# Keys and queries of the differential attention: turning two heads' fp32 rows at once and splitting them behind the turn, against splitting first and turning one head at a time

## What is computed

```
q = (x @ w_q).reshape(B, S, 2, H, Dh) * (Dh ** -0.5)      # H = 8 heads, two maps of Dh = 64
q1, q2 = partial_rope(q[:, :, 0]), partial_rope(q[:, :, 1])
a = softmax(q1 k1^T) - lam * softmax(q2 k2^T)              # causal
o = rms_norm(a @ v) * (1 - lambda_init);  return o @ w_out
```

## Time and profile before

| | |
|---|---|
| three runs | 1014.42 us median (1013.09 to 1014.72) |
| the profiled execution, its time | 1013.32 us |
| its span, first to last instruction | 1011.4 us |
| mean granted TensorE clock | 0.999 |
| busy: PE, DVE, ACT, POOL | 998.2, 664.6, 469.5, 103.7 us |
| differential attention from the query projection to its output | about 740 to 812 us of the span |

### The profile page before, as it was taken

The page is one execution under the profiler, slowest core; times in us unless marked ns, Lnnn a source line. Parts: engine busy times, 40 slices in busy tenths (PEclk is TensorE's granted clock), DMA queues, the critical chain, the costliest instruction groups (busy, mean ns, idle before and its releaser), DMA issues.

```text
span 1011.4 us, 13543 instructions
## 1 busy us (share of the span) xinstructions
PE 998.2 (99%) x5374; PEld 850.5 (84%) x5374; DVE 664.6 (66%) x653; ACT 469.5 (46%) x632; POOL 103.7 (10%) x141
## 2 busy tenths in 40 slices
PE   9999999999999999999999999999998999999997
PEld 7888888888888888888888888888887788888885
DVE  5876763765856667674575567774598877677544
ACT  7544433444864544343443444333468655434430
POOL 0020000222920100000022000000033110000000
PEclk9999999999999999999999999999999999999999
DMA  9866554560223755554447664654459366555431
GB/s 333 295 213 223 199 209 172 195 221 1 87 95 96 249 183 173 212 196 167 167 167 234 217 215 166 207 208 166 167 173 160 126 208 210 165 180 215 146 123 42
DMA packets 80060, 181.58 MB, mean 180 GB/s; under 512 B 3392, under 2 KB 9680, under 8 KB 80016
## 3 DMA queue, kind: packets, MB, share of 16 engines
q1 hardware_dynamic: 73312, 170.21, 48.4%
q0 software_dynamic: 6704, 10.76, 4.4%
HBM read 177.81 MB, written 1.05 MB: 177 GB/s over the span
## 4 chain that ended last, share of the span: by engine, by line
PE 94%; DVE 2%; ACT 2%; DMA 0%; issue 0%; POOL 0%; POOLq 0%; SPq 0%; DVEq 0%; ACTq 0%
PE acc L1479 15%; PE acc L1481 15%; PE acc L1480 15%; PE acc L1579 13%; PE aux L1579 7%; PE acc L1581 7%; PE trb L1579 6%; PE trb L1529 4%; PE aux L1581 4%; PE trb L1581 3%; PE acc L1737 1%; PE acc L1600 1%; PE acc L1597 1%; PE acc L1601 1%; PE aux L1781 1%; ACT norm_gb L782 1%
## 5 line engine op out<-in xcount | busy, mean ns | idle before, releaser
L968 DVE TENSOR_TENSOR w_lo<-raw,w_hi 128x2048 fp32r<-128x2048 f32 x148 | 336.6, 2283 | 174.0 <-ACT w_hi L674 173.9
L674 ACT ACTIVATE w_hi<-raw 128x2048 fp32r<-128x2048 f32 x148 | 280.3, 1902 | 152.4 <-PE acc L1481 124.3
L1579 PE MATMUL acc<-xt,w_hi 128*128 128x512 f32 x576 | 205.0, 395 | 0.0
L1581 PE MATMUL acc<-xt,w_lo 128*128 128x256 f32 x576 | 161.6, 280 | 0.0
L1479 PE MATMUL acc<-w_hi,ht_hi 128*128 128x512 f32 x352 | 137.0, 389 | 0.0
L1481 PE MATMUL acc<-w_hi,ht_lo 128*128 128x512 f32 x352 | 136.8, 389 | 0.0
L1480 PE MATMUL acc<-w_lo,ht_hi 128*128 128x512 f32 x352 | 136.8, 389 | 0.0
L1579 PEld LDWEIGHTS acc<-xt,w_hi 128*128 128x128 f32 x576 | 108.0, 187 | 25.4
L1479 PE MATMUL acc<-w_hi,xt 128*128 128x512 f32 (+1 forms) x320 | 127.3, 398 | 0.2 <-DVE xt L983 0.2
L1481 PE MATMUL acc<-w_hi,xt 128*128 128x512 f32 (+1 forms) x320 | 123.5, 386 | 0.0
L1480 PE MATMUL acc<-w_lo,xt 128*128 128x512 f32 (+1 forms) x320 | 123.4, 385 | 0.0
(11 more groups left out here) (233 smaller groups left out, 1306.8 us busy)
## 6 DMA issues: line engine op xcount, KB each, us to landing
raw<-ffn_gate_up SPq DMA_DIRECT2D x84, 1024.0 KB, 5.2
raw<-ffn_w_down SPq DMA_DIRECT2D x44, 1024.0 KB, 4.9
raw<-w_kv SPq DMA_DIRECT2D x8, 1024.0 KB, 6.2
raw<-w_in SPq DMA_DIRECT2D x6, 1024.0 KB, 5.2
raw<-ffn_gate_up SPq DMA_DIRECT2D x16, 256.0 KB, 6.1
raw<-w_out_a SPq DMA_DIRECT2D x4, 1024.0 KB, 6.0
raw<-w_q SPq DMA_DIRECT2D x4, 1024.0 KB, 5.1
raw<-w_out_b SPq DMA_DIRECT2D x4, 1024.0 KB, 5.5
```

What stands on the lines that cost most here:

```text
L674: act.activation(w_hi[:, slot, 0:k * c], raw[:, slot, 0:k * c], ACT.Copy).then_inc(hi_ready, 1)
L968: dve.tensor_tensor(w_lo[:, slot, 0:k * c], raw[:, slot, 0:k * c], w_hi[:, slot, 0:k * c].bitcast(F32), ALU.subtract).then_inc(lo_ready, 1)
L1579: pe.matmul(bank.rearrange("p (a s) -> p a s", a=2), hi[:, k, cols], xt[:, :, kt, :], start=(kt == 0), stop=False)
L1581: ins = pe.matmul(bank[:, 0:SEQ], lo[:, k, cols], xt_hi[:, kt, :], start=False, stop=(kt == KT - 1))
```

## The change

The rotated fp32 rows are turned as they are, two maps of 64 in one 128x128 block, so a turn of four blocks now carries 8 maps, and there are 8 turns in place of 16. `split_beside` is gone for keys and queries of this mixer. Behind a turn `stacked_high` has ACT write the high parts out of PSUM, in two instructions of 64 partitions (the even maps lie on the upper 64 partitions, the odd ones on the lower 64), and `stacked_low` has DVE write the low parts in two more, each onto the other 64 partitions of the same slot; only then is the bank freed. For odd maps the high part now lies on the lower 64 partitions, in keys and queries alike. `dq` is now `y`, the mixer's output keeps `k_nat` under the name `diff_o`, and a small product moves within `y`. Late turns are one at step 2 and one at step 6, behind the turn of the probabilities; the queries of tile 0 are all turned before the loop. PE's early turns stand before k-steps 1 and 3 of both units of four k-steps, then before query pieces 1 and 3.

```diff
-DIFF_EARLY = [("kr", tok, part) for tok in range(TOKS) for part in range(4)] + [("qr", 0, 0), ("qr", 0, 1)]
-DIFF_LATE = {0: ((("qr", 0, 2),), (("qr", 0, 3),)), 2: ((("qr", 1, 0),), (("qr", 1, 1),)),
-             6: ((("qr", 1, 2),), (("qr", 1, 3),))}
+DIFF_EARLY = [("kr", 0, 0), ("kr", 0, 1), ("kr", 1, 0), ("kr", 1, 1), ("qr", 0, 0), ("qr", 0, 1)]
+DIFF_LATE = {2: ("qr", 1, 0), 6: ("qr", 1, 1)}
...
+        dq = y
+        diff_o = k_nat
+        def stacked(heads, part, tok):
+            at = [(slice(8 * part + r, 8 * part + 8, 2), slice(tok * P, (tok + 1) * P)) for r in range(2)]
+            top, low = slice(0, DH), slice(DH, P)
+            return [(top, heads[top, at[0][0], at[0][1]], heads[low, at[0][0], at[0][1]]),
+                    (low, heads[low, at[1][0], at[1][1]], heads[top, at[1][0], at[1][1]])]
...
             def swap_keys(tok):
                 for half in range(2):
-                    for part in (2 * half, 2 * half + 1):
-                        t = TURN_OF["kr", "diff", tok, part]
-                        pool.wait_ge(tr_free[t % 2], t // 2 + 1)
+                    t = TURN_OF["kr", "diff", tok, half]
+                    pool.wait_ge(tr_free[t % 2], t // 2 + 1)
...
+            def stacked_high(name, tok, part):
+                t = TURN_OF[name, "diff", tok, part]
+                act.wait_ge(tr_full, t + 1)
+                turned = trb[:, t % 2].rearrange("p (k c) -> p k c", c=P)
+                for at, hi, lo in stacked({"kr": dks[:, 0], "qr": dqs[:]}[name], part, tok):
+                    ins = act.activation(hi, turned[at], ACT.Copy)
+                ins.then_inc(tr_hi, 1)
+            stacked_high("kr", 0, 0)
+            split_parts(n0 + 4, (0,))
+            stacked_high("kr", 0, 1)
+            split_parts(n0 + 4, (1,))
+            stacked_high("kr", 1, 0)
+            split_parts(n0 + 4, (2,))
+            stacked_high("kr", 1, 1)
+            split_parts(n0 + 4, (3,))
+            stacked_high("qr", 0, 0)
+            split_parts(n0 + 5, (0, 1))
+            stacked_high("qr", 0, 1)
+            split_parts(n0 + 5, (2, 3))
             for i, sc, tr, pv in job_steps(DIFF_JOBS):
-                for name, tok, part in DIFF_LATE.get(i, ((), ()))[0]:
-                    copy_keys_or_queries(name, tok, part)
                 if sc:
                     exps("diff", DIFF_JOBS, i, len(NSA_JOBS))
                 if tr:
                     copy_joined(i - 2)
+                if i in DIFF_LATE:
+                    stacked_high(*DIFF_LATE[i])
...
+            def stacked_low(name, tok, part):
+                t = TURN_OF[name, "diff", tok, part]
+                dve.wait_ge(tr_hi, SPLIT_OF[name, "diff", tok, part] + 1)
+                turned = trb[:, t % 2].rearrange("p (k c) -> p k c", c=P)
+                for at, hi, lo in stacked({"kr": dks[:, 0], "qr": dqs[:]}[name], part, tok):
+                    ins = dve.tensor_tensor(lo, turned[at], hi.bitcast(F32), ALU.subtract)
+                ins.then_inc(tr_free[t % 2], 1)
...
-            split_beside(4)
             diff_queries_out(0, 0)
...
             diff_queries_out(0, 1)
-            split_beside(5)
-            copy_heads("kr", 0, 1)
+            stacked_low("kr", 0, 0)
...
             split_parts(n0 + 4, (0,))
-            copy_heads("kr", 0, 3)
-            split_beside(6)
+            stacked_low("kr", 0, 1)
             split_parts(n0 + 4, (1,))
-            copy_heads("kr", 1, 1)
+            stacked_low("kr", 1, 0)
             diff_queries_out(1, 0)
             split_parts(n0 + 4, (2,))
-            copy_heads("kr", 1, 3)
-            split_beside(7)
+            stacked_low("kr", 1, 1)
             split_parts(n0 + 4, (3,))
-            copy_heads("qr", 0, 1)
-            split_beside(8)
+            stacked_low("qr", 0, 0)
             split_parts(n0 + 5, (0,))
+            stacked_low("qr", 0, 1)
...
-                for name, tok, part in DIFF_LATE.get(i, ((), ()))[1]:
-                    copy_heads(name, tok, part)
-                if i == 5:
-                    split_beside(9)
+                if i in DIFF_LATE:
+                    stacked_low(*DIFF_LATE[i])
                 if i == 2:
                     diff_queries_out(1, 1)
...
-            def diff_turn(name, tok, part):
-                k, at = (4 + tok, part) if name == "kr" else (6 + 2 * tok + part // 2, part % 2)
-                pe.wait_ge(beside_ready, k + 1)
-                turn((name, "diff", tok, part), [beside[k][:, 4 * at + j].rearrange("p s d -> p (s d)").bitcast(F32)
-                                                 for j in range(4)])
+            def diff_turn(name, tok, half):
+                pe.wait_ge(rope_done, 5 + tok if name == "kr" else 7 + 2 * tok + half)
+                src = {"kr": k_nat, "qr": dq}[name][:, tok, half * 512:(half + 1) * 512]
+                turn((name, "diff", tok, half), [src[:, j * P:(j + 1) * P] for j in range(4)])
```

More of the change, by code:

```diff
@@ L185, in count_events @@
             for i, _, tr, pv in job_steps(DIFF_JOBS):
-                first, second = DIFF_LATE.get(i, ((), ()))
-                turn.extend([(name, "diff", tok, part) for name, tok, part in first])
                 if tr:
                     turn.append(("p", "diff", i - 2))
-                turn.extend([(name, "diff", tok, part) for name, tok, part in second])
+                if i in DIFF_LATE:
+                    name, tok, half = DIFF_LATE[i]
+                    turn.append((name, "diff", tok, half))
                 if i in TILE0_DONE["diff"]:
@@ L197, in count_events @@
     return unit, fill, {name: i for i, name in enumerate(turn)}, {
-        name: i for i, name in enumerate([t for t in turn if t[0] in "xh"])}
+        name: i for i, name in enumerate([t for t in turn if t[0] in "xh" or t[1] == "diff" and t[0] in ("kr", "qr")])}
 UNIT_OF, FILL_OF, TURN_OF, SPLIT_OF = count_events()
@@ L318, in build_program @@
         beside = [v[:, a:a + 2 * DH * h].rearrange("p (h s d) -> p h s d", s=2, d=DH) for v, a, h in (
[L319 to L321 removed]
+            (flat(nqs), 0, 4), (flat(nqs), 2048, 4), (flat(w1v).bitcast(F32R), 0, 16), (flat(xt_lo), 0, 16))]
         rotated = [kv_a[:, tok, KS:KS + 512].rearrange("p (m g d) -> p m g d", m=2, d=DH)[:, :, 0:2, :]
[L323 to L326, removed]
+                   for tok in range(TOKS)] + [nq[:, tok, :].rearrange("p (h d) -> p h d", d=DH) for tok in range(TOKS)]
+        def stacked(heads, part, tok):
[3 more added lines that the diff above has]
+                    (low, heads[low, at[1][0], at[1][1]], heads[top, at[1][0], at[1][1]])]
         x_raw = k_nat[:].rearrange("p t (k s) -> p (t k) s", s=SEQ)
@@ L905, in _ @@
             n0 = UNIT_OF["diff_q"]
-            for k in range(4, 6):
-                split_beside(k)
             x_high("ffn2", 1)
@@ L1440, in diff_norm @@
                 tok, g = DIFF_TURNS[turn]
-                o, to = acc[:, 2 + turn % 2], dq[:, tok, g * 512:(g + 1) * 512]
+                o, to = acc[:, 2 + turn % 2], diff_o[:, tok, g * 512:(g + 1) * 512]
                 dve.wait_ge(rms_pow, turn + 1)
@@ L1945, in _ @@
             copied("x", "ffn2", 1, 1)
-            run_units(1, n0, (1,), columns_unit, inner={0: {k: early[2 + k] for k in range(4)}})
+            run_units(1, n0, (1,), columns_unit, inner={0: {1: early[2], 3: early[3]}})
             query_piece(0)
-            early[6]()
-            early[7]()
+            early[4]()
             query_piece(1)
-            early[8]()
             query_piece(2)
-            early[9]()
+            early[5]()
             query_piece(3)
@@ L1993, in _ @@
                     tok, half = i // 4 > 0, int(i in (2, 8))
-                    for m in range(2):
-                        copied("qr", "diff", int(tok), 2 * half + m)
+                    copied("qr", "diff", int(tok), half)
                     for t in range(tok + 1):
@@ L2006, in _ @@
                            lambda h, m, part: dks[:, part, map_slot(h, m)])
-                for t in DIFF_LATE.get(i, ((), ()))[0]:
-                    diff_turn(*t)
                 for kt in DIFF_QUERY_STEPS.get(i, ()):
@@ L2017, in _ @@
                                                 for j in ((0, 1) if tok else (0, 2))])
-                for t in DIFF_LATE.get(i, ((), ()))[1]:
-                    diff_turn(*t)
+                if i in DIFF_LATE:
+                    diff_turn(*DIFF_LATE[i])
                 if pv >= 0:
@@ L2024, in _ @@
                     pe.wait_ge(turn_mixed, len(NSA_TURNS) + half + 1)
-                    turn_wide(("x", "diff_o", 0), dq[:, 0, :], [half])
+                    turn_wide(("x", "diff_o", 0), diff_o[:, 0, :], [half])
             for kt in (5, 6):
```

25 lines of the change are left out of this document (3 added, 22 removed).

## The result

Five runs of the changed kernel took 1021.83 us in the median (1020.26 to 1023.92), five of the kernel before beside them 1014.72 (1013.09 to 1015.1): a ratio of 1.0066, 95% interval 1.0051 to 1.0081, or 7.1 us slower. The forecast was +4.5 us and 1018.4 us, with 1020.4 as the upper end of its range. The direction was right, the size too small, and the measured time lies outside the range. The profiled execution took 1020.26 us, its span is 1018.4.

The account below looks back on a forecast made before the run. PE, 99% busy, was taken as the bound, ACT and DVE from 770 to 785 us. PE saves 3.5 us but idles 8.0 more: +4.5 on 1013.32 gives 1017.8, with half of 1.1 1018.4 us; range 1013.8 to 1020.4.

Parts of the forecast that it names:

- The term for the clock: Granted clock under 1.00 from 770 to 790 us would add to the loss; nothing for it in the sum.
- PE saves 3.5 us: Eight turns fewer (16 to 8) at 0.44 us each take 3.5 us off PE, taken as the bound.
- the -3.5 of the rival: Faster rival's limit: with all waits covered, PE's whole saving comes through, -3.5 us; rival's chance 0.10.
- 64 partitions at the full price: New ACT and DVE splits of 64x512 cost as much as 128x512: about 0.60 and 0.69 us.
- the faster and the level rivals: Faster than before: splits at half time or less, chance 0.10. Level: 0.6 to 0.9 of the price, -1.2 to +1.7, 0.18.
- The hold on DVE: DVE instructions alternating between halves lose overlap, stepping 0.70 us, not 0.61; sum 4.5 us with it, 2.8 without.
- The walk: Engine lists timed from 749.5 us: scores 0 0.95 us late, scores 4 2.2, values 4 4.5.
- ACT at 0.50 a step: ACT's split instructions step 0.50 us with overlap; upper bound 0.60 without any overlap, giving +5.1.
- From there on the shift stays: Behind values 4 no engine's list differs, so the 4.5 us delay stays unchanged to the end.
- The key DMAs: Eight key DMAs cost nothing: the last four start 0.4 us later, landing by some 775 us, before scores 4.
- The level of the runs: Median of three runs was 1.1 us above the profiled execution; half was added, giving 1018.4 us.
- slower than forecast: Rival: ACT loses its overlap too (+5.1) or key DMA landing delays scores (some +6); 1019.5 to 1020.5, chance 0.10.

Follow-up runs that it names:

- before, half turns: Kernel before the change, with key and query turns of two blocks instead of four, half the turned blocks left out; stretch -2.14 us, ratio 0.9979.
- fill: Changed kernel with 23 idle bf16 matmuls on PE, ahead of scores 4, the turn in step 4 and values 4; stretch +5.01 us, ratio 1.0047.
- after: The changed kernel, unaltered; ratio 1.0066; stretch (last turn of x beside query projection to turns of mixer output, tile 1) 61.23 us, before 54.40.
- norm_first: Changed kernel with DVE's diff_norm of step 6 moved ahead of the low pair of qr(1,1); stretch +6.54 us, ratio 1.0047.
- same_half: Changed kernel with both instructions of each pair reading the upper half of PSUM, lower half left out; stretch +5.84 us, ratio 1.0049.
- wide: Changed kernel with one instruction of 128 partitions and 1024 elements per engine and turn, low part overwriting high; stretch +3.37 us, ratio 1.0029.
- after, again: The changed kernel, unaltered, run and profiled a second time in another group; stretch +6.27 us, 1022.5 us against 1014.91, ratio 1.0073.
- wide_fill: Changed kernel with one 128-partition, 1024-element instruction per engine and turn, plus idle matmuls (4, 3 and 9) in PE's long waits; stretch +1.80 us, ratio 1.0016.
- same_half_fill: Changed kernel with pairs reading only PSUM's upper half, plus idle bf16 matmuls in PE's three long waits; stretch +3.51 us, ratio 1.0033.

## Why the prediction was too low

Two of its steps failed. The term for the clock was put at nothing, and it cost 1.3 to 1.8 us. And ScalarE's pair was priced at 0.50 us a step with overlap, where it took 0.60 without; with VectorE's holds in front of the pairs this made the waits some 0.5 us longer than forecast. The mechanism of the waits was right. All its steps, one by one:

- **PE saves 3.5 us.** As busy time yes, 32 blocks are gone. As time at the end it was worth 2.1 in the old arrangement, without any new cost (before, half turns). For the -3.5 of the rival, waits of the kernel before would have had to go too.
- **64 partitions at the full price.** Right: 593 and 689 ns, means of L916 and L1367, near the 594 and 686 to 692 of the earlier trace rows. With that the faster and the level rivals fell.
- **The hold on DVE.** Right at 1.42 us a pair. The walk allowed some 0.25 us for all holds behind other instructions; the four steps of 0.70 to 0.79 instead of 0.61 came to 0.49.
- **ACT at 0.50 a step.** This term of the sum was wrong. The actual step is 0.60 and more, the instruction behind the pair included: the upper bound ("no overlap at all", +5.1) was the truth. The only rows of a change of halves, VectorE's, pointed to it, though nothing then showed that ScalarE does the same. With the clock taken out (fill) the stretch is +5.01, within 0.1 us of that bound and 0.5 over the forecast; and 0.5 us is what scores 0 were late beyond the walk, at a clock of 1.00 (1.43 against 0.95). The split of this half microsecond between ScalarE's step and VectorE's holds was not measured.
- **The clock.** The prediction named it as what would add to the loss, and left it out of the sum because before had kept 1.00 with 2.6 us of idle PE in 15. But that idle time was many waits of under 1 us. The forecast itself put 2.2 us of delay and a long wait at scores 4 and 2.5 us at values 4; these are what the clock fell behind (in the second execution of after only the first of them). The four pairs with and without idle matmuls (after, norm_first, same_half, wide) give 1.3 to 1.8, 1.65, 2.33 and 1.57 us. This is the larger part of what was missing.
- **The walk.** Scores 0 came 1.43 us late from the first row (766.52 - 749.82 against 764.82 - 749.55) for 0.95, scores 4 2.79 for 2.2, values 4 5.81 for 4.5. "From there on the shift stays" was wrong: it grew to 6.83, in the matmuls at 1.2 GHz behind values 4 (in after, again and in fill, with the clock at 1.00 there, it did not grow). The prediction had said that a shift at 812 us other than at values 4 would put the cause in the output stage; it was not there, since the stretch ends before it.
- **The key DMAs** were not in the way: scores 4 start at 777.77, 0.05 us behind the end of VectorE's low part (776.33 + 1.39), and same_half, where that part ends earlier, has them 1.3 us earlier.
- **The level of the runs.** Half of 1.1 us was taken; the kernel before stood at 1014.72 us beside the changed one, 0.8 above the 1013.9 on which 1018.4 rests. The rival "slower than forecast" was not added up the same way: +5.1 and +6 on 1013.9 are 1019.0 and 1019.9, not 1019.5 and 1020.5, which count the whole 1.1.

The sum as the runs have it, in the stretch: -2.1 for the turns that PE no longer does, 3.9 for the bank's longer way (from -2.14 to wide_fill's +1.80), 1.7 for two instructions of 64 partitions in place of one of 128, with the holds around VectorE's pairs (to same_half_fill), 1.5 for the change of halves within the pairs (to fill), 1.3 to 1.8 for the clock. The first step of this chain compares versions of two different kernels, so 3.9 is a difference and not a cost measured by itself. Behind the stretch, the way from the output's first turn to the next turn of `x` took 8.08 us in the kernel before, 7.96 in one execution of the kernel after (811.05 to 819.01) and 8.58 in the other; why is open, and no kernel was made for it.

## What to carry to other kernels

An engine that shows 99% busy over the span may still have a stretch in which two elementwise engines set the time, and taking work from it there in exchange for a longer way through them can lose twice: as waits, and as matmuls at the lower clock behind a long wait. Here the clock fell behind most of the waits of 1.3 to 2.7 us, and behind none of up to 1.0 us before the loop. So price such a forecast wait on PE together with the matmuls behind it, as a range. And let instructions on half the partitions stay on one half, on ScalarE as on VectorE, or use one instruction over 128 partitions.

## What the runs showed of the hardware

- ScalarE holds an instruction whose partitions start in the other half: pairs of 64x512 took 1.20 us across halves (after) and 1.06 on one half (same_half), the follower starting 1.23 and 0.96 us behind the pair's start.
- Instructions of 64 partitions cost as much as those of 128: 593 against 594 ns on ScalarE, 689 against 686 to 692 on VectorE, each with 512 elements a partition.
- The granted clock fell from 1.00 to 0.50 behind PE waits of 1.5 and 2.7 us (after) in a stretch where PE had shorter waits as well, for some 3 to 6 us. In one execution it stayed at 1.00 behind a wait of 2.72. With 23 idle bf16 matmuls in the waits (fill) it was 1.00 in every window read, and the stretch was shorter by 1.3 to 1.8 us.
- The same program, executed twice, lost its clock twice in one execution (0.77 and 0.89 in the windows from 770 to 785 and from 785 to 800) and once in the other (0.83 and 0.94).
